# Token-major residual and 512-wide matmuls in a two-block hybrid model, with two token tiles staggered over the norms

## What is computed

```python
def first_block(x, ...):
    h = rms_norm(x, norm1_w); proj = h @ w_in                  # 1024 -> 7168
    # retention over 64-token chunks, gated linear recurrence (LRU), both gated
    mix = sigmoid(..) * y_a + sigmoid(..) * y_b                # y_a, y_b end in 1024x1024 products
    x = x + mix @ w_out
    up = rms_norm(x, norm2_w) @ ffn_w_up; gate, val = split(up, [3072])
    gate = causal_depthwise_conv(gate, 3 taps)                 # along the tokens
    x = x + (gelu(gate) * val) @ ffn_w_down
    return rms_norm(x, norm_f_w)

def second_block(x, ...):                                      # two layers
    h = (silu(n @ w_gate) * (n @ w_up)) @ w_down               # n = rmsnorm(x, g[0]), hidden 2816
    x = x + 0.5 * rmsnorm(h, g[1])
    x = x + rmsnorm(hybrid_mixer(rmsnorm(x, g[2])), g[3])      # gated linear attention, conv, window attention
    h = swiglu_ffn(rmsnorm(x, g[4]), ...)
    x = x + 0.5 * rmsnorm(h, g[5])
```

## Time and profile before

| | |
|---|---|
| runs | 1589.17, 1591.98, 1592.87 us |
| profiled execution, first to last instruction (span) | 1590.1 us |
| median of the runs less this span | 1.9 us |
| PE / weight loads / DVE / ACT / POOL busy | 97 / 95 / 70 / 45 / 11% |
| DMA | 252 MB, 159 GB/s over the span |
| mean granted clock of TensorE | 0.976 of full |

### The profile page before, as it was taken

One profiled execution on the slowest core, in us unless ns is written; L12 is line 12 of the kernel. 1 busy time (PEld: TensorE's weight loads), 2 busy tenths in 40 slices (PEclk: granted clock), 3 DMA queues, 4 the chain that ended last, 5 costly groups with the idle time before them and its releaser, 6 DMA issues.

```text
span 1590.1 us, 31272 instructions
## 1 busy us (share of the span) xinstructions
PE 1535.1 (97%) x12682; PEld 1514.0 (95%) x12682; DVE 1110.1 (70%) x1446; ACT 720.8 (45%) x908; POOL 181.6 (11%) x191
## 2 busy tenths in 40 slices
PE   6999999999999999999789999999999987999998
PEld 5999999999999999999779999999999986999998
DVE  6766786677744766567977767567665699776654
ACT  4433853555533444434335544445443424454442
POOL 0000000000001000012904000010000264300000
PEclk8999999999999999999879999999999997999999
DMA  8544455566555566555116665656655540556661
GB/s 267 195 133 133 159 188 184 155 178 179 181 179 159 148 180 181 192 159 125 62 59 154 181 181 183 195 135 185 185 187 170 133 133 1 160 160 182 180 195 51
DMA packets 378774, 252.28 MB, mean 159 GB/s; under 512 B 24371, under 2 KB 377924, under 8 KB 378692
## 3 DMA queue, kind: packets, MB, share of 16 engines
q1 hardware_dynamic: 377808, 248.54, 53.0%
q10 hardware_dynamic: 884, 2.58, 0.5%
HBM read 250.04 MB, written 1.05 MB: 158 GB/s over the span
## 4 chain that ended last, share of the span: by engine, by line
PE 83%; DVE 13%; ACT 2%; issue 1%; DMA 1%; SPq 0%; ACTq 0%; DVEq 0%
PE stream L1429 57%; PE psm L1429 23%; DVE w_lo L789 3%; DVE yc L1246 3%; PE ps L1429 3%; ACT w_hi L480 2%; DVE s_gla L1258 1%; DMA raw<-in_w_in 1%; DVE x L867 1%; DVE hn L857 1%; DVE a_lo L835 0%; DVE ss L1273 0%; DVE sq L1330 0%; DVE pt L879 0%; DVE yc L1243 0%
## 5 line engine op out<-in xcount | busy, mean ns | idle before, releaser
L1429 PE MATMUL stream<-a_hi,w_hi 128*128 128x256 f32 x2464 | 707.6, 287 | 12.4 <-DVE a_lo L820 9.1
L1429 PE MATMUL stream<-a_lo,w_hi 128*128 128x256 f32 x2464 | 701.2, 285 | 0.0
L1429 PE MATMUL stream<-a_hi,w_lo 128*128 128x256 f32 x2464 | 700.9, 284 | 0.0
L789 DVE TENSOR_TENSOR w_lo<-raw,w_hi 128x2048 fp32r<-128x2048 f32 x240 | 552.5, 2303 | 175.7 <-ACT w_hi L480 175.6
L480 ACT ACTIVATE w_hi<-raw 128x2048 fp32r<-128x2048 f32 x240 | 457.1, 1907 | 235.9 <-PE psm L1429 153.7
L1429 PEld LDWEIGHTS stream<-a_hi,w_hi 128*128 128x128 f32 x2464 | 476.6, 193 | 18.5 <-issue 9.8
L1429 PEld LDWEIGHTS stream<-a_lo,w_hi 128*128 128x128 f32 x2464 | 477.1, 194 | 0.0
L1429 PEld LDWEIGHTS stream<-a_hi,w_lo 128*128 128x128 f32 x2464 | 476.9, 194 | 0.0
L1429 PE MATMUL psm<-h_hi,w_hi 128*128 128x256 f32 x896 | 251.7, 281 | 0.0
L1429 PE MATMUL psm<-h_lo,w_hi 128*128 128x256 f32 x896 | 251.7, 281 | 0.0
L1429 PE MATMUL psm<-h_hi,w_lo 128*128 128x256 f32 x896 | 251.7, 281 | 0.0
(11 more groups left out here) (246 smaller groups left out, 1525.4 us busy)
## 6 DMA issues: line engine op xcount, KB each, us to landing
raw<-in_ffn_w_up SPq DMA_DIRECT2D x136, 512.0 KB, 5.1
raw<-in_ffn_w_down SPq DMA_DIRECT2D x104, 512.0 KB, 3.7
raw<-in_ffn_w_gate SPq DMA_DIRECT2D x88, 512.0 KB, 4.0
raw<-in_w_in SPq DMA_DIRECT2D x80, 512.0 KB, 4.6
raw<-in_w_out SPq DMA_DIRECT2D x24, 512.0 KB, 4.0
raw<-in_w_in SPq DMA_DIRECT2D x20, 256.0 KB, 4.6
raw<-in_w_ret_o SPq DMA_DIRECT2D x8, 512.0 KB, 4.0
raw<-in_w_lru_o SPq DMA_DIRECT2D x8, 512.0 KB, 4.3
```

What stands on the lines that cost most here:

```text
L789: V.tensor_tensor(w_lo[s][:, :, :], raw[s][:, :, :], w_hi[s][:, :, :].bitcast(F32), ALU.subtract).then_inc(w_split, 1)
L1429: return nc.tensor.matmul(dst, lhs, rhs, start=start, stop=stop, skip_group_check=True)
```

## The change

The residual lies token-major now: `x_t`, two tiles of 128 tokens x 1024. Four kinds of product become token-major too, the out projections and down projections, and in the second-kind feed-forwards gate and up: 128 tokens of the activation are stationary, 512 columns of weight move (`wide_pass`). Such a unit holds 4 k-tiles x 512 columns and is used in two passes, one for each token tile, of 12 matmuls each (24 where it was 48); a down unit with the last two k-tiles of 22 is a half one. The gated product comes out token-major and must be feature-major for down, so four PE transposes turn it for each pair of units (`turn_hidden`), 11 pairs a feed-forward. The first block's input projections, its up projection and the mixers' projections stay feature-major, 256 wide.

The last three units of a stage with passes (HELD) are run first for tile 0, all three, then for tile 1; the first three of the next feed-forward the same (`tail_passes`, `head_passes`). A norm is done for each token tile: the square sums come from ACT's accumulator (`y_square`, `x_square`), the scale is one value a partition, and eight PE transposes per tile (`turn`) give the feature-major operand, which ACT and DVE scale and split from PSUM in pieces of 128 columns (`turned_hi`, `turned_lo`). Mean squares by PE, sums by POOL and the fillers of the norms are gone; those inside the mixer stay. Gain rows are loaded by SP (`load_gain`, 4 KB spread over the partitions). The table `ret_d` is loaded later, into `hn`. All hardware loops are written out. The final transposes and copies are gone.

```diff
+HELD = 3
...
+def tail_passes(units):
+    both, last = units[:-HELD], units[-HELD:]
+    return [(c, t) for c in both for t in range(TT)] + [(c, t) for t in range(TT) for c in last]
...
+def head_passes(units):
+    first, both = units[:HELD], units[HELD:]
+    return [(c, t) for t in range(TT) for c in first] + [(c, t) for c in both for t in range(TT)]
...
-        x = sb("x", [P, KT, T])
+        x_t = sb("x_t", [P, TT, D])
...
+            def y_square(c, t, n, scale):
+                act.wait_ge(unit_used, DONE[c, t])
+                junk_free()
+                count["y"] += 1
+                nc.scalar.activation(junk[:, 0:512], y_bank(t, n), ACT.Square, scale=scale,
+                                     accum_out=ms4[:, 2 * t + n:2 * t + n + 1]).then_inc(y_squared, 1)
...
+            def turned_hi(i, t, group, col):
+                for h in range(2):
+                    act.wait_ge(xt_full, x_count(i, t, h))
+                    for k in range(4 * h, 4 * h + 4):
+                        at = k % 4 * P
+                        ins = nc.scalar.activation(a_hi[:, k, t * P:t * P + P], xt_bank(t, h)[:, at:at + P], ACT.Identity,
+                                                   scale=vecs[:, group, col + k:col + k + 1])
...
+            hi(U1_OUT + 2)
+            hi(U1_OUT + 3)
+            x_half_square(1, 0, 0)
+            x_half_square(2, 0, 1)
+            hi(U1_UP)
+            turned_hi(N_UP1, 0, 0, V1["norm2"])
+            hi(U1_UP + 1)
+            x_half_square(3, 1, 0)
+            x_half_square(4, 1, 1)
+            hi(U1_UP + 2)
+            turned_hi(N_UP1, 1, 0, V1["norm2"])
...
+                for j in range(NF2):
+                    g = j // 2
+                    if j % 2:
+                        for t in range(TT):
+                            act.wait_ge(unit_used, DONE[c0 + j, t])
+                            act.wait_ge(rstd_ready, root_count(norm_of(f), False, t))
+                            nc.scalar.activation(th_t[:, 2 * (g % 2) + t, :], up_bank(g, t)[:, 0:UC], ACT.Tanh,
+                                                 scale=rs4[:, 2 + t:3 + t]).then_inc(th_ready, 1)
+                    hi(c0 + j + 3)
+                    if j % 2 == 0 and g:
+                        pair_hi(g - 1)
...
+            def between(i, last, scale, group=None, col=None, next_scale=None):
+                y_square(last, 0, 1, scale)
+                hi(last + 1)
+                if group is not None:
+                    turned_hi(i, 0, group, col)
+                hi(last + 2)
+                y_square(last, 1, 1, scale)
+                if group is not None:
+                    x_square(i, 0, next_scale)
+                hi(last + 3)
+                if group is not None:
+                    turned_hi(i, 1, group, col)
+                    x_square(i, 1, next_scale)
...
+            add_half(U1_OUT + 2, 0, 0)
+            add_half(U1_OUT + 3, 0, 1)
+            two_halves(2, 0, 2, RMS_EPS)
+            scaled(0)
+            lo(U1_UP)
+            turned_lo(N_UP1, 0, 0, V1["norm2"])
+            add_half(U1_OUT + 2, 1, 0)
+            lo(U1_UP + 1)
+            add_half(U1_OUT + 3, 1, 1)
+            two_halves(2, 1, 4, RMS_EPS)
+            scaled(1)
+            lo(U1_UP + 2)
+            turned_lo(N_UP1, 1, 0, V1["norm2"])
...
+            add_half(U1_DOWN + 5, 0, 0)
+            add_half(U1_DOWN + 5, 1, 0)
+            for d in range(6, 9):
+                lo(U1_DOWN + d + 3)
+            add_half(U1_END - 1, 0, 1)
+            two_halves(0, 0, 7, RMS_EPS)
+            dve.wait_ge(gain_loaded, 16)
+            final_norm(0)
+            lo(U1_END)
+            turned_lo(N_F, 0, 2, 0)
+            lo(U1_END + 1)
+            add_half(U1_END - 1, 1, 1)
+            next_variance(N_F, 0, 4 * RMS_EPS)
+            two_halves(0, 1, 8, RMS_EPS)
+            final_norm(1)
+            lo(U1_END + 2)
+            turned_lo(N_F, 1, 2, 0)
+            next_variance(N_F, 1, 4 * RMS_EPS)
...
+                def gate(g, t):
+                    at = 2 * (g % 2) + t
+                    dve.wait_ge(th_ready, NF1 + NF2 * f + 2 * g + t + 1)
+                    link(V.scalar_tensor_tensor(out=ab[:, t, :], in0=th_t[:, at, :], scalar=1.0, in1=up_bank(g, t)[:, 0:UC],
+                                                op0=ALU.add, op1=ALU.mult))
+                    V.scalar_tensor_tensor(out=hb[:, at, :], in0=ab[:, t, :], scalar=r_sq[:, t:t + 1],
+                                           in1=up_bank(g, t)[:, UC:2 * UC], op0=ALU.mult, op1=ALU.mult).then_inc(pair_gated, 1)
+                def pair_lo(g):
+                    dve.wait_ge(h_hi_ready, NF1 + NG * f + g + 1)
+                    V.tensor_tensor(h_lo[:, 2 * g:2 * g + 2, :], pair2(h_bank(g)), h_hi[:, 2 * g:2 * g + 2, :].bitcast(F32),
+                                    ALU.subtract).then_inc(h_split, 1)
+                for j in range(NF2):
+                    g = j // 2
+                    if j % 2:
+                        for t in range(TT):
+                            if g == 0:
+                                square_of_root(t, i - 1)
+                            gate(g, t)
+                    lo(c0 + j + 3)
+                    if j % 2 == 0 and g:
+                        pair_lo(g - 1)
...
+            def between(i, last, at, group=None, col=None, next_eps=None):
+                squared = y_squares(i)
+                two_halves(0, 0, squared + 3, 4 * RMS_EPS)
+                at[0].append(gained(0, 1, squared + 3))
+                residual(i, 0, at[0])
+                lo(last + 1)
+                if group is not None:
+                    turned_lo(i, 0, group, col)
+                lo(last + 2)
+                if group is not None:
+                    next_variance(i, 0, next_eps)
+                two_halves(0, 1, squared + 4, 4 * RMS_EPS)
+                at[1].append(gained(1, 1, squared + 4))
+                residual(i, 1, at[1])
+                lo(last + 3)
+                if group is not None:
+                    turned_lo(i, 1, group, col)
+                    next_variance(i, 1, next_eps)
...
+            def wide_pass(c, t, dst, hi_t, lo_t, ks, first, last, ready=None):
+                split_unit(c)
+                tok = slice(t * P, t * P + P)
+                h, l = wide(w_hi[c % NS]), wide(w_lo[c % NS])
+                for n, k in enumerate(ks):
+                    if ready:
+                        ready(k)
+                    begin, end = first and n == 0, last and n == len(ks) - 1
+                    mm(dst, hi_t[:, k, tok], h[:, n, :], begin, False)
+                    mm(dst, hi_t[:, k, tok], l[:, n, :], False, False)
+                    ins = mm(dst, lo_t[:, k, tok], h[:, n, :], False, end)
+                end_pass(ins, c, t)
...
+            def turn(i, t, src):
+                for h in range(2):
+                    pe.wait_ge(x_ready, x_count(i, t, h))
+                    for n in range(4):
+                        k = 4 * h + n
+                        ins = nc.tensor.transpose(xt_bank(t, h)[:, n * P:n * P + P], src[:, t, k * P:k * P + P], ident)
+                    ins.then_inc(xt_full, 1)
...
-            def norm(p7):
-                keep_warm(2)
-                mean_squares(p7)
-                keep_warm(10)
-                inverse_rms()
-                keep_warm(20)
...
+            def turn_hidden(f, g):
+                pe.wait_ge(pair_gated, NF2 * f + 2 * g + 2)
+                if g > 1:
+                    pe.wait_ge(h_split, NF1 + NG * f + g - 1)
                 for n in range(2):
-                    split_unit(c + n)
-                    bank_free(g + n)
-                for k in order:
-                    ready(k)
-                    for n in range(2):
-                        ins = feature_major((c + n) % NS, banks[n], tiles[n], hi_t, lo_t, k == order[0], k == order[-1], kts=(k,))
-                        if k == order[-1]:
-                            ins.then_inc(unit_used, 1)
-
-            def third_unit(c, g, bank, p7):
-
-                mean_squares(p7)
-                split_unit(c)
-                bank_free(g)
-                feature_major(c % NS, bank, BOTH[0:1], a_hi, a_lo, True, False)
-                inverse_rms()
-                feature_major(c % NS, bank, BOTH[1:2], a_hi, a_lo, False, True).then_inc(unit_used, 1)
-
-            def ffn(c, g, bank0, norm_no, h0, p7):
-                two_units(c, g, [stream[(bank0 + n) % 3] for n in range(2)], a_hi, a_lo, a_ready(norm_no))
-                third_unit(c + 2, g + 2, stream[(bank0 + 2) % 3], p7)
-                hidden(c + 3, 0, g + 3, 0, stream[bank0])
-                with pe.Fori(0, (NF2 - 4) // 3) as i:
-                    for j in range(4, 7):
-                        hidden(c + j, i, g + j, i * 3, stream[(bank0 + j) % 3])
-                down(c + NF2, g + NF2, NF2, h0)
+                    for t in range(TT):
+                        ins = nc.tensor.transpose(h_bank(g)[:, n * T + t * P:n * T + t * P + P],
```

(33 more changed lines are left out.)

876 lines of the change are left out of this document (428 added, 448 removed).

## The result

The changed kernel takes 1563.05 us (median of 4, 1561.05 to 1563.43) against 1592.42 before: ratio 0.9816, 95% interval 0.9802 to 0.9829. The forecast was 1518, the range 1500 to 1556. The direction was right, and of a gain of 74 us 29 came. By number alone rival (e), 1560, lay nearest, then rival (a), 1554; which of them was the case has to come from the traces.

A forecast was written before the change was run, and what follows sets the result against it. Bound taken: number of matmuls times their pace, plus what stands between stages. Terms -81.6 + 21.6 - 12.9 - 1.0 = -73.9 turn 1590.1 into 1516.2, shown as median 1518 us; range 1500 to 1556.

The forecast's parts named there:

- rival (e): Weight operands: they come late from DMA or the conversions; between 1518 and 1590, most likely 1560 us; chance 0.04.
- rival (a): Wide matmuls: each keeps the narrow one's 13 ns loss, 0.2266 us; +36, 1554 us; chance 0.12.
- Part 1: Up/gate, down and out projections: half as many matmuls, 512 wide, at 0.217 us each; -81.6 us.
- What holds it is the stationary load: Narrow 256-column matmuls: load (0.111 us) nearly equals columns (0.107), so each loses 12 to 13 ns.
- the plain F32 product of the retention: Nearest trace row for a wide matmul: its long records take 0.217 us, load hidden nearly whole; taken as the pace.
- Part 2: Feed-forward hidden tile: 176 added transposes at 0.11 us plus changes of kind, without waiting for the gating; +21.6 us.
- Part 3: Norms per token tile, partly hidden under held passes, exposed before mixers and first up; -12.9 us together, ends -20 and +9.
- Part 4: Start of the kernel: retention table no longer fetched while the first weight unit lands, -1 us; other changes 0.
- (b): Norms give nothing back: stalls on conversions everywhere, clock down after each; +20, 1538 us; chance 0.17.
- (c): Turn of the hidden tile becomes the loop, transposes waiting 2 us per pair; +88, 1606 us; chance 0.04.
- (d): Only loads count, not columns: wide matmuls run at the narrow 0.120 us; -363, 1155 us; chance 0.01.
- The marks: Signs to check: wide pace 0.215 to 0.219, transposes without wait, pauses 8 to 10 us, TensorE idle not over 60 us.

The follow-up runs named there:

- e1_pace: Kernel of matmul blocks alone, no other engine working: fp32r at 512 columns starts every 0.2267 us, with operands 128 bytes apart 0.2324 to 0.2333, bfloat16 0.2160.
- e2_pad: Changed kernel with only an unused 128-byte tile ahead of the stage tiles, aligning h_hi and h_lo with the other operands: 1553.9 us, ratio 0.9756.
- e13: Kernel before with two unused tiles (64 and 224 bytes), putting moving activations 192 bytes past the weights: 1554.4 us over six runs, ratio 0.976.
- e9_align: Matmul blocks alone, moving tile shifted against stationary by 0 to 224 bytes: 512 columns 0.2271 at 0, 0.2333 at 128; 256 columns 0.1200 at 0, 0.1133 at 192.
- e12_shifts: Blocks of 48 fp32r matmuls alone, moving tile shifted in 16-byte steps: at 256 columns 112 and 192 bytes are fast; no 512-column block under 0.231.
- e16: Changed kernel with every wide matmul cut in two and the weights 192 bytes past the activations and h: 1555.1 us, ratio 0.9782.

## Why the prediction was wrong

- **Part 1, the pace: the step that failed is "What holds it is the stationary load", with the choice of 0.217 by "the plain F32 product of the retention".** A wide matmul, whose columns take nearly twice the 0.111 us in which a load and 128 columns follow each other, still lost 13.3 ns (e1_pace), and the F32 row stood for another kind, which loses 2.5. The upper bound, 0.2133 + 0.0133, was the value. The 128-column row showed only how fast a load and 128 columns can follow each other, not that the load made the loss at 256. In the sum: 3744 x (0.2267 - 0.217) = +36 us, 1554. The Trainium skill's 215.7 ns at 512 columns (TensorE: Matmul & The Clock Gate, "Wait — 56ns, not 53.3ns?") is what bfloat16 did here (216.0), not what fp32r does.
- **A term that was missing:** the down projections' 0.2326 to 0.2333, 1344 x 0.006 = +8 us, from h's place (e2_pad took it away). With both terms, 1518 + 36 + 8 = 1562; measured 1563. Part of this closeness is luck, for the remaining differences below, of up to 3 us each, nearly cancel.
- **Part 2:** right. 0.44 a turn against 0.49 costed, 0.49 with the slow dozen behind; without a wait but at the first pair of each feed-forward, 0.8 us each, 3.1 together. A turn's price on the path was confirmed by doubling it.
- **Part 3:** right in mechanism, and nearly in size. The pauses were 8.4 (mixer) and 9.1 us (286.4 to 295.5, first up) against 8.5 and 9.8, with the clock at 0.50 to 0.6 behind them. Waits for `w_lo` in the feed-forward heads came as named, 0.5 and 1.5 us in layer one's second feed-forward, where the kernel before ran through the earlier trace rows. The stagger's worth was tested (20 us). To take a norm by itself, the stages on both sides of it are counted together and their matmuls and turns taken off at the paces above. A norm behind a layer's out projection then costs 5.9 us (8.4 before; forecast 5.7), the one between the layers 4.7 (8.3; 5.3), the first block's last 8.6 (8.7; 8.7), the end 6.1 (12.7; 6.0). Out projection, norm and first up together stayed as they were, where +1.2 was forecast. The two norms ahead of the mixers came out 1.6 and 1.9 dearer than before, where +0.1 each was forecast. The 7 us that the table shows for the mixers are mostly this cut: 2.4 and 2.0 of them lie in the projections, whose third unit no statistic interrupts any longer; the other 2.5 are the end of the first mixer, 30.2 us before and 27.7 after, which scatters as much between kernels of the same code and is no gain of the change.
- **Part 4:** not tested. The table has -1.4 against -1, but in eight profiles of kernels with the changed kernel's start this stretch takes 263.6 to 267.2 us, and 265.0 in the one of the kernel before.
- **Rivals.** (a) was the case, plus the place of h. Its 0.12 was too low: no row of this type spoke for the lower bound against the upper. (b) did not happen: the norms gave back nearly what was forecast. (c): 3.1 us of waits in the turns, not 88. (d): no. (e) has the nearest number, but the waits for `w_lo` are 8.4 us in all, and most of them stand in the heads, where they had been costed.
- **The marks** were right on the pace (0.22 or over: wrong), on the transposes and the pauses. The mark on TensorE's idle sum pointed the right way by luck: it is 82 us (55 before), over the 60 named, but although the norms gained and not because the pace was wrong; the fillers had counted as busy.

What stays open: why fp32r loses 13.3 or 6.7 ns, and by what rule the addresses and the start of a phase choose between them. No run here shows it.

## What to carry to other kernels

Price a new form of matmul from a row of the same type, and measure a block of it alone when half the sum rests on it: taking the wrong one of two bounds was 36 of the 45 us of error. In fp32r, try the place of the stationary and moving tiles (a few unused bytes) before rebuilding a kernel for width: 288 bytes brought 38 us, the rebuilding 29, and on top of good places 14. Such a kernel has to be timed several times: one of e13's six runs took 22 us more than the others. When a chain is exposed, move the conversions behind it and fill the pause, both together.

## What was not expected of the hardware

- fp32r from start to start in us, per place of the moving tile past the stationary one: 256 columns 0.120 (0 bytes), 0.1167 to 0.120 (others), 0.1133 (192, 112); 512 columns 0.2267 (0), 0.229 (64), 0.231 to 0.2345 (others). bfloat16 takes 0.216 at 512 columns, at 0 and at 128 bytes (e1_pace, e9_align, e12_shifts).
- The pace settles: after a change of kind it takes some 12 matmuls (a turn in the changed kernel), and one address pattern has two steady paces, 0.1133 and 0.1178, each kept through a phase of hundreds of matmuls (e13, e16).
- An unused tile of 128 bytes moved this kernel by 9 us, two of 64 and 224 bytes the one before by 38.
